# Four projection units that the prompt block no longer stores, and that the first latent block splits and stores instead

## The reference, cut to what matters

```python
def _mixer(h, grid, s0f, s0b, w_in, ...):
    proj = jnp.einsum('btd,dc->btc', h, w_in)      # D_MODEL = 1024, all float32
    q, k, v, r, zf, zb, ga, gg = jnp.split(proj, [o1, o2, o3, o4, o5, o6, o7], axis=-1)
    ...
    of, sf = _gla_scan(qh, kh, vh, heads(gf), s0f)
    ...
    u = ga * jax.nn.sigmoid(gg)
    u = _depthwise_conv(...)                        # 31 taps
    ...
    out = jnp.einsum('btc,cd->btd', jnp.concatenate([o, u], axis=-1), w_out)
```

## Time and profile before

| | |
|---|---|
| time, median of 3 runs (lowest to highest) | 2453.41 us (2450.36 to 2458.17) |
| the profiled execution | 2452.26 us, span 2450.5 us, granted TensorE clock 0.954 |
| PE busy | 2262.2 us, 92% of the span |
| DVE busy | 1647.4 us, 67% |
| ACT busy | 1187.6 us, 48% |
| POOL busy | 732.1 us, 30% |
| DMA | 505.91 MB, mean 206 GB/s |
| window 40 to 150 us (prompt block) | PE 77.43 of 110 us busy, DVE 84.04, ACT 66.42, DMA engines 0.90 busy, 329 GB/s |
| window 150 to 325 us (end of the prompt block, first latent block) | PE 167.13 of 175 us, DVE 148.65, ACT 92.39, DMA 0.68 |

### The profile page before, as it was taken

How to read it: one execution, slowest core, us unless ns; L and a number is a source line. 1 busy time by engine, 2 the same in 40 slices (tenths; PEclk the granted TensorE clock), 3 DMA queues, 4 the chain that set the end, 5 groups by cost and what they waited for, 6 DMA issues and landing times.

```text
span 2450.5 us, 43730 instructions
## 1 busy us (share of the span) xinstructions
PE 2262.2 (92%) x16682; PEld 2063.5 (84%) x16682; DVE 1647.4 (67%) x2833; ACT 1187.6 (48%) x1933; POOL 732.1 (30%) x666
## 2 busy tenths in 40 slices
PE   4779999999997899966999999999999999999994
PEld 3768878788885677742999999999999999999994
DVE  1797979799788766438566656666566665666575
ACT  3746364553524444420655554555545555455652
POOL 1000000000001311100354455544555445554352
PEclk8889999999997999985999999999999999999997
DMA  7976676757737566353566677666776667766785
GB/s 233 377 271 219 211 242 232 258 191 268 229 125 255 179 192 198 107 161 97 164 192 188 189 208 204 192 185 191 207 205 195 181 192 206 205 196 182 271 266 193
DMA packets 281301, 505.91 MB, mean 206 GB/s; under 512 B 25793, under 2 KB 224318, under 8 KB 265312
## 3 DMA queue, kind: packets, MB, share of 16 engines
q1 hardware_dynamic: 241872, 377.94, 47.0%
q0 software_dynamic: 39312, 126.38, 19.2%
HBM read 405.74 MB, written 98.53 MB: 206 GB/s over the span
## 4 chain that ended last, share of the span: by engine, by line
PE 58%; DVE 4%; DMA 3%; ACT 2%; POOL 1%; issue 1%; SPq 1%; DVEq 0%; ACTq 0%; POOLq 0%
PE bank L1579 18%; PE bank L1581 18%; PE bank L1580 18%; DMA out_dram<-work_exp 1%; PE bank L1832 1%; PE bank L1898 1%; DVE work_exp L2733 1%; PE bank L1842 1%; PE bank L1850 1%; POOL x_rows L1518 1%; DMA work_exp<-x_rows 1%; ACT work_exp L1213 0%; DVE work_proj L2444 0%; PE bank L2055 0%; ACT hl_exp L1173 0%
## 5 line engine op out<-in xcount | busy, mean ns | idle before, releaser
L1579 PE MATMUL bank<-act_hl_exp,hl_exp 128*128 128x288 f32 x3072 | 911.8, 297 | 15.6 <-DVE hl_exp L2887 7.5
L1580 PE MATMUL bank<-act_hl_exp,hl_exp 128*128 128x288 f32 x3072 | 908.9, 296 | 0.0
L1581 PE MATMUL bank<-act_hl_exp,hl_exp 128*128 128x288 f32 x3072 | 907.4, 295 | 0.0
L1579 PEld LDWEIGHTS bank<-act_hl_exp,hl_exp 128*128 128x128 f32 x3072 | 579.2, 189 | 16.9 <-DVE hl_exp L2887 8.5
L1581 PEld LDWEIGHTS bank<-act_hl_exp,hl_exp 128*128 128x128 f32 x3072 | 581.0, 189 | 0.0
L1580 PEld LDWEIGHTS bank<-act_hl_exp,hl_exp 128*128 128x128 f32 x3072 | 579.9, 189 | 0.0
L2887 DVE TENSOR_TENSOR hl_exp<-work_exp,hl_exp 128x1024 fp32r<-128x1024 f32 x192 | 231.3, 1226 | 217.8 <-ACT hl_exp L1173 217.8
L2887 DVE TENSOR_TENSOR hl_exp<-raw_exp,hl_exp 128x1024 fp32r<-128x1024 f32 x192 | 232.1, 1225 | 200.1 <-ACT hl_exp L1173 200.1
L2444 DVE SCALAR_TENSOR_TENSOR work_proj<-work_proj,wcv 128x392 f32<-128x392 f32 (+11 forms) x600 | 337.3, 635 | 0.6
L1173 ACT ACTIVATE hl_exp<-work_exp 128x1024 fp32r<-128x1024 f32 x192 | 199.2, 1055 | 211.5 <-PE bank L1581 205.5
L1173 ACT ACTIVATE hl_exp<-raw_exp 128x1024 fp32r<-128x1024 f32 x192 | 198.6, 1052 | 166.0 <-PE bank L1581 166.0
(11 more groups left out here) (367 smaller groups left out, 3274.3 us busy)
## 6 DMA issues: line engine op xcount, KB each, us to landing
hl_proj<-park_w POOLq DMA_DIRECT2D x80, 1024.0 KB, 6.3
raw_exp<-in_w_e_gate_dram SPq DMA_DIRECT2D x32, 1024.0 KB, 5.9
raw_exp<-in_w_e_up_dram SPq DMA_DIRECT2D x32, 1024.0 KB, 5.9
work_exp<-in_w_e_gate_dram SPq DMA_DIRECT2D x32, 1024.0 KB
work_exp<-in_w_e_up_dram SPq DMA_DIRECT2D x32, 1024.0 KB, 6.0
raw_exp<-in_w_e_down_dram SPq DMA_DIRECT2D x32, 1024.0 KB, 7.2
work_exp<-in_w_e_down_dram SPq DMA_DIRECT2D x32, 1024.0 KB, 6.6
park_w<-hl_proj SPq DMA_DIRECT2D x10, 2048.0 KB, 13.0
```

Source lines behind the costliest of these rows:

```text
L1579: pe.matmul(out, lh, rh, start=first, stop=False)
L1580: pe.matmul(out, lh, rl, start=False, stop=False)
L1581: return pe.matmul(out, ll, rh, start=False, stop=last_)
```

## The change

Units 2, 3, 4 and 5 are no longer stored by the prompt block. The prompt block gives units 2 and 5 a third slot, `spare_hl`, made of the columns of `h_hl` that 256 tokens don't use; unit 3 then goes to slot 0, unit 4 to slot 1. `proj_hi` of units 2, 5, 6 and 7 waits for no store any more, that of units 3 and 4 for the stores of units 0 and 1, that of 8 and 9 for those of 6 and 7. The first latent block loads units 2 to 5 raw again (L543), splits them and stores them; ACT does their high parts, POOL their low parts (`pool_lo`, L1403). POOL also takes half 1 of units 7, 8 and 9 of the prompt block from DVE (`POOL_LO = 7`). The raw loads of units 2 and 3 of the latent block are issued at the end of the prompt block. In the first latent block POOL's load of unit 6 waits for the store of unit 4, and that of unit 7 for the store of unit 5.

```diff
+RESPLIT = (2, 3, 4, 5)
+SPL_EXP = NPROJ + len(RESPLIT)
+POOL_LO = 7
...
+        spare_hl = h_hl[:, :, :, TP:BT]
...
+        def again(b, j):
+            return not b.prompt and b.i == 0 and j in RESPLIT
+        def w_part(b, j, q, part_):
+            if b.prompt and j in (2, 5):
+                return spare_hl[:, part_, :, 128 * q:128 * q + 128]
+            return hl[:, {3: 0, 4: 1}.get(j, j % 2) if b.prompt else j % 2, q, part_]
...
                 def weights(j):
-                    if not b.prompt:
-                        return
-                    sp.wait_ge(s_lo[j % 2], 2 * (j // 2) + 2)
-                    if j + 2 < NPROJ:
-                        load_proj(j + 2)
-                    sp.dma_start(park_w[j], hl[:, j % 2].bitcast(f32)).then_inc(s_wst[j % 2], 16)
+                    if b.prompt:
+                        sp.wait_ge(s_lo[j % 2], lo_count(b, j, 1))
+                        if j + 2 < NPROJ:
+                            load_proj(b, j + 2)
+                        else:
+                            load_proj(nb, j + 2 - NPROJ + RESPLIT[0])
+                    elif again(b, j):
+                        sp.wait_ge(s_lo[j % 2], lo_count(b, j, 1))
+                        if j + 2 in RESPLIT:
+                            load_proj(b, j + 2)
+                    if again(b, j) if not b.prompt else j not in RESPLIT:
+                        sp.dma_start(park_w[j], hl[:, j % 2].bitcast(f32)).then_inc(s_wst[j % 2], 16)
...
             def proj_hi(p, j):
-                if not p.prompt or j >= NPROJ:
+                if not p.prompt and not again(p, j):
                     return
-                if j >= 2:
-                    act.wait_ge(s_uh.sem, 2 * (j - 1))
-                    act.wait_ge(s_wst[j % 2], 16 * (j // 2))
-                act.wait_ge(s_raw[j % 2], 16 * (j // 2 + 1))
+                if p.prompt and j >= 3:
+                    act.wait_ge(s_uh.sem, 2 * (j - 2 if j < 8 else j - 1))
+                elif not p.prompt:
+                    p.wait(act, s_uh, 2 * (j - 1))
+                if p.prompt and j in (3, 4):
+                    act.wait_ge(s_wst[1 - j % 2], 16)
+                elif p.prompt and j >= 8:
+                    act.wait_ge(s_wst[j % 2], 32)
+                elif not p.prompt and j >= 4:
+                    act.wait_ge(s_wst[j % 2], 64)
+                act.wait_ge(s_raw[j % 2], raw_count(p, j))
...
+            def pool_lo(b, j, q):
+                pool.wait_ge(s_hi, hi_count(b, j, q))
+                pool.tensor_tensor(hl[:, j % 2, q, 1], raw[:, j % 2, :, 128 * q:128 * q + 128],
+                                   hl[:, j % 2, q, 0].bitcast(f32), ALU.subtract).then_inc(s_lo[j % 2], 1)
...
             def stage2(b, nb):
+                for j in range(POOL_LO if b.prompt else NPROJ, NPROJ):
+                    pool_lo(b, j, 1)
                 if not b.prompt:
                     for j in range(2, NPROJ):
+                        if again(b, j):
+                            pool_lo(b, j, 0)
+                            pool_lo(b, j, 1)
+                            continue
+                        if b.i == 0 and j in (6, 7):
+                            wait_alone(pool, s_alone, s_wst[j % 2], 80)
                         next_w(b, j, 0)
                         next_w(b, j, 1)
...
-                for q in range(2):
-                    dve.wait_ge(s_hi, 2 * j + q + 1)
+                for q in range(1 if j >= POOL_LO else 2):
+                    dve.wait_ge(s_hi, hi_count(p, j, q))
```

More of the change, by code:

```diff
@@ L1585, in proj_half @@
                 s = j % 2
-                if b.prompt:
-                    pe.wait_ge(s_lo[s], 2 * (j // 2) + q + 1)
+                if b.prompt or again(b, j):
+                    pe.wait_ge(s_lo[s], lo_count(b, j, 1 if b.prompt and j >= POOL_LO else q))
                 else:
-                    b.wait(pe, s_w[s][q], 16 * (j // 2 + 1))
+                    pe.wait_ge(s_w[s][q].sem, w_count(b, j))
                 proj_part(b, j, q, 0, KC, 0, b.T).then_inc(s_uh.sem, 2 if b.prompt and (j, q) == (9, 1) else 1)
@@ L1594, in proj_part @@
                 for k in range(k0, k1):
-                    w = hl[:, j % 2, q, :, k, :]
-                    last = three(psum[2 * (j % 2) + q][:, t0:t1], w[:, 0], w[:, 1], h_hl[:, 0, k, t0:t1],
+                    w = [w_part(b, j, q, i)[:, k, :] for i in range(2)]
+                    last = three(psum[2 * (j % 2) + q][:, t0:t1], w[0], w[1], h_hl[:, 0, k, t0:t1],
                                  h_hl[:, 1, k, t0:t1], k == 0, k == KC - 1)
@@ L1728, in latent_rest @@
                     mod_pair(b, 0)
-                b.wait(pe, s_w[0][0], 16 * 5)
+                pe.wait_ge(s_w[0][0].sem, w_count(b, 8))
                 b.wait(pe, s_v, 1)
@@ L1748, in latent_rest @@
                     mod_pair(b, 1)
[L1749 removed]
+                pe.wait_ge(s_w[1][1].sem, w_count(b, 9))
                 b.wait(pe, s_v, 4)
```

41 lines of the change are left out of this document (24 added, 17 removed).

## The result

The changed kernel takes 2475.57 us (median of 4 runs, 2474.69 to 2480.84) against 2453.07 us before: a ratio of 1.0093, 95% interval 1.0081 to 1.0105. The forecast was 2458 with a range up to 2466. The profiled execution took 2475.7 us, its span is 2474.0 us and its mean granted clock 0.949.

The account below looks back on a forecast made before the run. DVE was taken to bound the prompt block, and PE to have almost no slack in the first latent block. Latent +8.0 less prompt 3.3 gave +4.7 us: 2458 against the median, own range 2454 to 2461, overall 2444 to 2466.

Parts of the forecast that it names:

- the prompt block up to its masks: Prompt block: earlier weights, fewer halves on DVE and DVE's standstill beside POOL sum to -3.3 us at PE's masks.
- POOL's three halves: Prompt block: each half moved to POOL holds DVE about 2.0 us, so the three cost DVE 6.0 us.
- so the whole of it reaches the first latent block: End of prompt block: PE waits for the masks, so the full 3.3 us gain carries into the next block.
- the modulation: First latent block: ACT's modulation delays PE's transposes of tile 2 from 233.29 to 236.6; PE loses 3.3 us.
- unit 5's low part: First latent block: POOL's two halves alternate with DVE's products of 2.28 us and end at about 240.
- The chain: First latent block: unit 5's store must land before unit 7's weights load into its slot, costing PE another 4.7 us.
- store, then load: First latent block: a long store of unit 5 delays unit 7's load; time 2461 to 2466, chance 0.24.
- POOL free: Both blocks: POOL's halves cost DVE nothing, the prompt block gives 9.3 us; time 2444, chance 0.14.
- Scans not held: First latent block: DVE's scans run unhindered beside POOL; net -0.7 us, time 2453, chance 0.14.
- the waits only change names: Prompt block: ACT waits for raw loads instead of stores, DVE gains nothing, latent 8.0 us stays; 2461, chance 0.05.

## Why the prediction was wrong

**Right: the prompt block up to its masks.** Forecast -3.3 us at PE's masks, measured -3.4. The parts fit too: -4.85 at the sigmoid for -4.3, unit 4's raw load ended ACT's wait at 82.6 for 82.2. POOL's three halves were to cost DVE 6.0; they cost 2.2 at the first (14 taps in 7.75 us), 1.3 at L2518 and 2.1 at L2496, 5.5 in all, while the 21 taps in between weren't held.

**Wrong: "so the whole of it reaches the first latent block".** 0.7 of 3.4 us did. I followed PE and DVE to the masks and stopped. Behind them ACT's gate reuses a row buffer, and the row's store was in the queue behind transfers among which the change had put new raw loads. It was issued at 137.43 and landed at 154.6. The gate's slack was in no row that I read. Cost against the sum: 2.7 us.

**Too small: the modulation, 3.3 us, measured 5.7.** I counted three halves of 2.0 ahead of the difference; four met DVE there, two of them on copies of 0.19 us that took 2.21 and 2.32. A copy was held as long as a scan. Held 8.3 us instead of 6.0.

**The step that failed most: unit 5's low part "ends at about 240 on POOL, because its two halves alternate with DVE's products".** It ended at 251.01. In the kernel before, scans, small copies and differences of this stretch begin 0.03 us after the end of the row ahead, pauses enough for POOL each time; products and taps begin 0.08 us before it. When POOL asked for unit 5's first half, DVE had run for 12.1 us without a pause. The earlier trace rows show POOL let in or DVE held each time, and I took that for a rule of fairness. It cost two waits that aren't in the sum: 8.5 us of PE for the low part, and 2.6 for unit 6's weights, whose loads POOL could issue only behind its subtractions. Making the halves on DVE and pausing DVE both removed the first.

The Trainium skill, "SBUF — State Buffer", section "Who interferes with whom", says that whoever issues first gets the shared ports for the whole instruction and the other fully blocks; the trace agrees for one instruction (6.50 us for a scan of 4.42). For a stream it falls short: POOL was blocked for 12 us, by two products, a copy and 14 taps in turn.

**The chain, 4.7 us, measured 0.35.** PE waited only 0.35 us for unit 7's weights. The store of unit 5 took 9.3 us and not 13.0, but above all everything that asks for the weights was later than the chain: it started 11 us later than I had it, PE asked 18 us later. Where POOL makes no halves the same store costs 2.7 us. The rival "store, then load", with a long store, did not happen, although its range came nearest to the time; what was long were unit 6's loads.

**Not in the sum: the clock, 5.0 us.** I had PE's clock at 1.00 in the block and kept it there through 8 us of waits. Each long wait was followed by work at the lower level. The Trainium skill, "TensorE: Matmul & The Clock Gate", section "HAM oscillation — how this bites in real kernels", describes waits that leave the engine at the lower rate for the work behind them; the trace agrees (0.50 in 236.4 to 253.5 and in 267.1 to 270.5).

The sum by its own steps: prompt -0.7 for -3.3; latent block 5.7 + 8.5 + 2.6 + 0.35 + 5.0 = 22.1 for 3.3 + 4.7 = 8.0. That is +21.4; the span is 23.5 longer. Of the other 2.1 us, 1.5 are one step of the kind described above, between the third and the fourth latent block (143.2 for 141.7 us), which the change doesn't touch.

**The other rivals.** POOL free is refuted by the scans and by the kernel without POOL's halves. Scans not held is refuted by 6.50 against 4.42. That the waits only change names is half true: ACT waits 4.73 and 4.13 us for raw loads, yet the masks gain their 3.4.

## What to carry to other kernels

Work moved to GpSimd beside VectorE isn't free on either side: here each low half of 2.35 us held VectorE 2.1 us or stood still itself, for up to 12 us, and one that another engine waits for should not stand beside a run of independent VectorE instructions (a wait of VectorE for its own last result let it in here). A gain must be followed to the last reuse of a buffer before the next stage, small stores behind large transfers included. An engine that both computes and issues loads holds up the loads behind its computing, as unit 6's here. And a new TensorE wait of a few microseconds can cost more than its length: 22.1 us for 17.2 of waits here.

## What the runs showed of the hardware beyond what was expected

- A GpSimd subtraction can be kept out by a VectorE stream without pauses: 2.35 us became 7.18 beside 21 taps, and two took 16.60 beside products and 14 taps. With pauses put into VectorE's stream they took 2.59 and 7.65.
- In all traces here a subtraction that came at most 3.0 us behind VectorE's last pause got in at the next instruction boundary, and one that came 3.1 us or more behind it did not.
- A VectorE copy of 64x32 floats (0.19 us alone) took 2.2 to 2.3 us beside it, so this copy, with one SBUF input, was held too.
- A TensorE wait of 0.73 us was followed by a granted clock of 0.72 in one execution (325 to 330 us), and one of 0.75 us by 1.00 in another; the block took 143.2 and 141.7 us.
